# Transposes set inside the product ahead of them, later waits for joined branches, a rounding moved from GpSimd to VectorE, first refills in halves

## The reference

```python
h = _rmsnorm(x, g_mix[l])
rq, rk, rv, rg, nq, nk, nv, xq, gate_logits = jnp.split(h @ w_in[l], split_points, axis=-1)
y_ret = _retention_branch(rq, rk, rv, rg, ...)          # rotary q, k; (silu(rg) * group_norm(y)) @ w_ret_o
y_na = _neighbourhood_attention(nq, nk, nv, na_rpb[l]) @ w_na_o[l]
y_xa = _memory_cross_attention(xq, _rmsnorm(mem, g_mem[l]), w_mem_kv[l]) @ w_xa_o[l]
g_ret, g_na, g_xa = jnp.split(jax.nn.sigmoid(gate_logits), N_BRANCHES, axis=-1)
x = x + (g_ret * y_ret + g_na * y_na + g_xa * y_xa) @ w_out[l]
x = x + _hierarchical_moe(_rmsnorm(x, g_ffn[l]), ...)   # 4 groups x 4 experts, width 512, 2 per token
return _rmsnorm(x, g_final)
```

## Time and profile before

| what | value |
|---|---|
| median of 3 runs | 1771.41 us (1768.65 to 1774.07) |
| profiled execution, own time | 1773.05 us |
| its span, first to last instruction | 1771.3 us |
| PE busy | 1696.1 us (96%) |
| DVE, ACT, POOL busy | 326.0, 285.6, 64.7 us |
| DMA | 597.32 MB, mean 337 GB/s |
| mean granted clock of PE | 0.993 |

### The profile page before, as it was taken

How to read it: one execution, slowest core, us unless ns; L and a number is a source line. 1 busy time by engine, 2 the same in 40 slices (tenths; PEclk the granted TensorE clock), 3 DMA queues, 4 the chain that set the end, 5 groups by cost and what they waited for, 6 DMA issues and landing times.

```text
span 1771.3 us, 18844 instructions
## 1 busy us (share of the span) xinstructions
PE 1696.1 (96%) x8222; PEld 857.3 (48%) x8222; DVE 326.0 (18%) x770; ACT 285.6 (16%) x535; POOL 64.7 (4%) x92
## 2 busy tenths in 40 slices
PE   8999999989998999999998989999999999899996
PEld 7764443333433776543333333356544454565653
DVE  1340000000000325100000000031224132322222
ACT  2301110101010222110010101123240110122212
POOL 4000000000000101000000000040000000100000
PEclk9999999999999999999999999999999999899999
DMA  9878999999999936899999999995343426389996
GB/s 329 298 285 359 430 426 427 428 427 427 427 427 417 355 131 250 352 427 428 427 428 428 426 428 427 421 335 198 142 142 131 154 95 251 129 340 425 424 425 264
DMA packets 84498, 597.32 MB, mean 337 GB/s; under 512 B 5720, under 2 KB 14672, under 8 KB 51376
## 3 DMA queue, kind: packets, MB, share of 16 engines
q1 hardware_dynamic: 80848, 586.28, 81.5%
q0 software_dynamic: 3552, 9.65, 1.7%
HBM read 594.86 MB, written 1.05 MB: 336 GB/s over the span
## 4 chain that ended last, share of the span: by engine, by line
PE 66%; issue 18%; DMA 13%; DVE 1%; ACT 1%; POOL 0%; SPq 0%; POOLq 0%; DVEq 0%
PE psum L713 29%; PE psum L507 15%; DMA ring<-in_w_gate_dram 10%; PE psum L539 8%; DMA ring<-in_w_up_dram 3%; PE psum L701 3%; PE psum L746 2%; PE psum L546 2%; PE psum L566 1%; PE psum L662 1%; PE psum L579 1%; PE psum L594 1%; PE psum L767 1%; PE psum L499 1%; PE psum L606 0%
## 5 line engine op out<-in xcount | busy, mean ns | idle before, releaser
L713 PE MATMUL psum<-ring,xT 128*64 128x512 f32 (+1 forms) x2048 | 424.2, 562 | 35.6 <-DMA ring<-in_w_up_dram 18.8
L713 PEld LDWEIGHTS psum<-ring,xT 128*64 128x64 f32 x2048 | 147.0, 137 | 285.4 <-issue 248.9
L507 PE MATMUL psum<-ring,xT 128*128 128x512 f32 x592 | 258.5, 593 | 2.2 <-DVE work L2060 1.5
L713 PE MATMUL psum<-ring,work 128*64 128x512 f32 x1056 | 234.9, 593 | 2.9 <-ACT work L1355 1.4
L507 PEld LDWEIGHTS psum<-ring,xT 128*128 128x128 f32 x592 | 111.1, 190 | 136.9 <-issue 133.5
L1910 DVE TENSOR_TENSOR work<-work,psum 128x512 f32<-128x512 f32 (+1 forms) x48 | 43.5, 907 | 639.0 <-PE psum L713 639.0
L713 PEld LDWEIGHTS psum<-ring,work 128*64 128x64 f32 x1056 | 75.2, 137 | 147.6 <-issue 138.6
L539 PE MATMUL psum<-xT,ring 128*128 128x256 f32 x512 | 113.3, 380 | 1.5 <-DVE xT L1594 1.5
L1355 ACT COPY work<-psum 128x512 f32<-128x512 f32 (+1 forms) x48 | 24.7, 515 | 525.2 <-PE psum L767 525.2
L539 PEld LDWEIGHTS psum<-xT,ring 128*128 128x128 f32 x512 | 96.1, 190 | 15.0 <-DVE xT L1594 1.9
L1252 ACT ACTIVATE work<-psum 128x512 f32<-128x512 f32 (+1 forms) x86 | 49.5, 589 | 226.2 <-PE psum L507 119.0
(11 more groups left out here) (275 smaller groups left out, 1273.1 us busy)
## 6 DMA issues: line engine op xcount, KB each, us to landing
ring<-in_w_gate_dram SPq DMA_DIRECT2D x53, 2048.0 KB, 22.3
ring<-in_w_up_dram SPq DMA_DIRECT2D x53, 2048.0 KB, 24.4
ring<-in_w_down_dram SPq DMA_DIRECT2D x52, 2048.0 KB, 23.8
ring<-in_w_in_dram SPq DMA_DIRECT2D x16, 2048.0 KB, 9.7
ring<-in_w_exp_up_dram SPq DMA_DIRECT2D x16, 2048.0 KB, 20.6
ring<-in_w_exp_down_dram SPq DMA_DIRECT2D x11, 2048.0 KB, 22.3
work<-in_w_gate_dram SPq DMA_DIRECT2D x9, 2048.0 KB, 16.2
work<-in_w_exp_gate_dram SPq DMA_DIRECT2D x9, 2048.0 KB, 17.4
```

The source lines that it names most:

```text
L507: ins = pe.matmul(b[:, cols_at[0]:cols_at[1]], lhsT=lhsT(c), rhs=rhs(c), start=(c == order[0]), stop=(c == order[-1]))
L713: ins = pe.matmul(to[part * CAP:(part + 1) * CAP, 0:n], lhsT=lhsT, rhs=w[:, half * n:(half + 1) * n], start=first, stop=last)
```

## The change

Part 1, in block 2. `tile_around` is a product of one tile that calls `turns()` ahead of its chunk 6, so the transposes stand in the product's last quarter. It is used in three places: the turn of the normed input inside the product "xa", all four banks now of set v; the turn of y inside the last gate product, all of set v; and the turn of `comb` for t = 0 inside the third join, of set a (for t = 1 it stands between the first two tiles of "z", by `between`). The turns of q and k go ahead of the last "rg" tile, all of set a. `wait_made("joined")` of the second join now stands behind the rotary k's product; that of the third is replaced by waits for the tiles that a turn needs. DVE's and ACT's programs follow.

Part 2. `x_lo` is computed by DVE (`rounded_off`), and ACT's rounding `x_hi` moves ahead of its last copy.

Part 3, in all expert stages. The first refill that follows the first gate piece is loaded in halves: the first half when PE has done half of the piece's chunks (`half`), the second when all (`used`). To bring this forward the first gathers and the first gate chunks change order.

```diff
+            def tile_around(w, act, t, r, product, turns):
+                b = bank(r, product)
+                for c in range(DC):
+                    if c == 6:
+                        turns()
+                    ins = pe.matmul(b, lhsT=act[:, c, t * P:(t + 1) * P], rhs=w[:, c, :], start=(c == 0), stop=(c == DC - 1))
+                return full(r, ins)
...
-            freed[n] = nat(as_cols(n), memT, DC, 512, "a", "xa"); n += 1
-            turn(W(XA["H"], TC, D), DC, "xT", "mix")
+            w = as_cols(n)
+            tile(w, memT, DC, 512, 0, "a", "xa")
+            freed[n] = tile_around(w, memT, 1, "a", "xa", lambda: turn(W(XA["H"], TC, D), DC, "xT", "mix", rings="v")); n += 1
             wait_made("xT")
...
+            freed[n] = nat(as_cols(n), xT, DC, 512, "v", "rope"); n += 1
             wait_made("joined")
-            freed[n] = nat(as_cols(n), xT, DC, 512, "v", "rope"); n += 1
...
+            tile(as_cols(n), xT, DC, 512, 0, "a", "rg")
             wait_made("rope")
-            turn(W(RET["q"], TC, 512), 4, "rqk")
-            turn(W(RET["k"], TC, 512), 4, "rqk")
+            turn(W(RET["q"], TC, 512), 4, "rqk", rings="a")
+            turn(W(RET["k"], TC, 512), 4, "rqk", rings="a")
+            freed[n] = tile(as_cols(n), xT, DC, 512, 1, "a", "rg"); n += 1
...
-            turn(W(RET["y"], TC, D), DC, "oT", "gn")
+            tile(w, xT, DC, 512, 0, "a", "gate")
+            freed[n] = tile_around(w, xT, 1, "a", "gate", lambda: turn(W(RET["y"], TC, D), DC, "oT", "gn", rings="v")); n += 1
             wait_made("oT")
-            join(yT, DC, n); n += 2
-            wait_made("joined")
-            turn(W(W_COMB, TC, D), DC, "xT")
+            wait_made("gate")
+            freed[n] = nat(as_cols(n), yT, DC, 512, "v", "joined"); n += 1
+            w = as_cols(n)
+            tile(w, yT, DC, 512, 0, "v", "joined")
+            in_comb = made["joined_v"]
+            def comb_turned(t):
+                pe.wait_ge(S("joined_v"), in_comb + t)
+                turn(comb, DC, "xT", which=[t], rings="a")
+            freed[n] = tile_around(w, yT, 1, "v", "joined", lambda: comb_turned(0)); n += 1
...
+            def rounded_off(c):
+                dve.wait_ge(S("x_hi"), c + 1)
+                dve.tensor_tensor(x_lo[:, c, :], x[:, c, :], x_hi[:, c, :].bitcast(F32), ALU.subtract).then_inc(S("x_lo"), 1)
+            rounded_off(0)
+            turned_twice = lent[0] + 1
             b = borrow()
             dve.tensor_copy(xT[:, 0:4, P:2 * P], b.rearrange("p (a b) -> p a b", a=4)).then_inc(S("xT_v"), 1)
+            dve.wait_ge(S("a_full"), turned_twice)
+            rounded_off(1)
...
-                pool.tensor_tensor(x_lo[:, c, :], x[:, c, :], x_hi[:, c, :].bitcast(F32), ALU.subtract).then_inc(S("x_lo"), 1)
...
                     gather(0, 1, y_bank)
+                    pe.wait_ge(sem("xe"), plus(1, B["xe"]))
+                    up("gate", g_bank, 0, range(2))
                     gather(0, 2, u_bank)
                     pe.wait_ge(sem("xe"), plus(2, B["xe"]))
-                    up("gate", g_bank, 0, range(2))
+                    up("gate", g_bank, 0, range(2, 4))
                     gather(0, 3, m_bank)
-                    up("gate", g_bank, 0, range(2, 4))
                     pe.wait_ge(sem("xe"), plus(4, B["xe"]))
                     up("gate", g_bank, 0, range(4, DC))
...
+                    if early:
+                        sp.dma_start(ph.room(i)[:, 0:2048], half(0)).then_inc(sem("early"), 16)
+                        sp.wait_ge(sem("used"), B["used"] + 1)
+                        sp.dma_start(ph.room(i)[:, 2048:], half(1)).then_inc(sem("piece%d" % ph.place[i]), 16)
```

More of the change, by code:

```diff
@@ L325, in __init__ @@
                     self.landed.append(16 * uses[place])
+                self.split = self.last.index(0)
                 self.uses = {m: self.place.count(m) for m in order}
@@ L651, in by_tiles @@
                     for half, w in enumerate(ws):
+                        if between is not None and half != t:
+                            between() if half else wait_made("xT")
                         b = bank("v", product)
@@ L691, in experts, with gather @@
                 n_group = N_EXP // ph.group
-                def gather(g, part, to):
+                def gather(g, part, to, first=0, end=None):
                     pe.wait_ge(sem("pick"), plus(TC * (g + 1), B["pick"]))
@@ L697, in gather @@
                     terms = [(src, t) for t in range(TC) for src in ((x_hi, x_lo) if ph.group == 4 else (x,))]
-                    for c in range(n):
+                    for c in range(first, end or n):
                         at = (n * part + c) * P
@@ L707, in piece @@
                     pe.wait_ge(*ph.there(i, B))
+                    if i == ph.split and not ph.more:
+                        pe.wait_ge(sem("early"), B["early"] + 16)
                     return ph.room(i)
@@ L725, in up @@
                             ins.then_inc(sem("used"), 1)
+                        elif b == per // 2 - 1 and ph.at(matrix, e, q) == 0 and not ph.more:
+                            ins.then_inc(sem("half"), 1)
                 def down(e):
@@ L823, in experts @@
                     gather(0, 0, m_bank)
-                    gather(0, 1, y_bank)
+                    gather(0, 1, y_bank, 0, 2)
                     pe.wait_ge(sem("xe"), plus(1, B["xe"]))
-                    up("gate", g_bank, 0, halves[0])
+                    up("gate", g_bank, 0, range(2))
+                    gather(0, 1, y_bank, 2)
+                    up("gate", g_bank, 0, range(2, 4))
                     gather_next(-1)
@@ L1468, in _ @@
                 empty(W(XA["mv"], TC, 512)[:, c, :], "xa")
-            turn(xT, DC, "xT")
             qT = W(XA["qT"], 4, T)
@@ L1526, in _ @@
                 nat(v[:, :, half * 512:(half + 1) * 512], 512, "rv")
-            for half in range(2):
-                nat(rg[:, :, half * 512:(half + 1) * 512], 512, "rg", ACT.Silu)
-            turn(W(RET["qT"], 4, T), 4, "rqk")
-            turn(W(RET["kT"], 4, T), 4, "rqk")
+            nat(rg[:, :, 0:512], 512, "rg", ACT.Silu)
+            empty(rg[:, 0, 512:D], "rg", ACT.Silu)
+            for name in ("qT", "kT"):
+                for t in range(TC):
+                    empty(W(RET[name], 4, T)[:, :, t * P:(t + 1) * P], "rqk")
+            empty(rg[:, 1, 512:D], "rg", ACT.Silu)
             for h in range(RET_HEADS):
@@ L1535, in _ @@
                 nat(gate[:, :, half * 512:(half + 1) * 512], 512, "gate", ACT.Sigmoid)
-            turn(W(RET["yT"], DC, T), DC, "oT")
-            turn(xT, DC, "xT")
+            for t in range(TC):
+                for j in range(0, DC, 4):
+                    empty(xT[:, j:j + 4, t * P:(t + 1) * P], "xT")
             for c in range(TC):
@@ L1542, in _ @@
                 empty(xT[:, j:j + 4, 0:P], "xT")
+            for c in range(TC):
+                act.wait_ge(S("norm"), NORM_AT["ffn"] - TC + 1 + c)
+                act.copy(x_hi[:, c, :], x[:, c, :]).then_inc(S("x_hi"), 1)
             took[0] += 1
@@ L1545, in _ @@
             took[0] += 2
-            for c in range(TC):
-                act.wait_ge(S("norm"), NORM_AT["ffn"] - TC + 1 + c)
-                act.copy(x_hi[:, c, :], x[:, c, :]).then_inc(S("x_hi"), 1)
             routed(3)
@@ L2333, in load @@
                     i = ph.at(matrix, e, q)
-                    if ph.last[i] >= 0:
+                    early = i == ph.split and not ph.more
+                    if early:
+                        sp.wait_ge(sem("half"), B["half"] + 1)
+                    elif ph.last[i] >= 0:
                         sp.wait_ge(sem("used"), plus(ph.last[i] + 1, B["used"]))
@@ L2350, in load @@
                     else:
-                        for half, name in enumerate(("piece%d" % ph.place[i], "tail")):
-                            part = src[:, half] if src.shape[1] > 1 else src[:, 0, half * 2048:(half + 1) * 2048]
-                            sp.dma_start(ph.room(i)[:, half * 2048:(half + 1) * 2048], part).then_inc(sem(name), 16)
+                        for k, name in enumerate(("piece%d" % ph.place[i], "tail")):
+                            sp.dma_start(ph.room(i)[:, k * 2048:(k + 1) * 2048], half(k)).then_inc(sem(name), 16)
                 for q in range(ph.nq):
```

51 lines of the change are left out of this document (24 added, 27 removed).

## The result

The changed kernel takes 1760.01 us (median of 4 runs, 1758.17 to 1761.67), the kernel before beside it 1771.01 (4 runs, 1768.65 to 1774.07): a ratio of 0.9937, 95% interval 0.9924 to 0.995, or 11.0 us less. In a later comparison it was 1759.94 against 1770.43, ratio 0.9944 (0.9931 to 0.9958). Faster was right, and 1760.0 lies in the range. But the forecast of 1764.0 stood for 7.5 us, a third too little, so the question behind the result is which term was too small.

What follows compares the result with a forecast made beforehand. DMA bounds the expert stages, PE block 2, and a PE, DVE and ACT chain runs up to phase 2's first refill. 5.1 + 2.55 - 0.75 + 0.2 + 0.4 = 7.5 us gained, so 1764.0; range 1758.5 to 1769.5.

Steps and rivals of the forecast that it cites:

- Part 1: Block 2: PE's waits at turns and joins shrink or go, 5.1 us gained, bounds 4.0 and 6.0.
- Part 2: Router: without POOL's subtractions DVE's steps are short and the choice comes 2.55 us earlier, bounds 0.2 and 2.6.
- The new order of gathers: Phase 2: new PE wait for ACT behind the fourth gather part, 0.75 us lost; no wait added in phases 0 and 1.
- The halves: Expert stages' first refill: an earlier half piece gains 0.2 us in all, bounds -2.7 and 7.4.
- The gap is moved, not closed: Phase 0 stream: half a piece fills the dip at 142, but the stream then stands dry from about 147.
- the 7.4 of the upper bound: Most the halves could gain: 1.05 MB at 428 GB/s, 2.45 us in each of three expert stages.
- My condition for being wrong: Signs: phase 0 or 1 ends over 1 us earlier, DVE late for logits, or longer DMA waits in the last stage.
- Rival B: Expert stages: the earlier half starts the whole stream earlier, 2 us or more per stage, about 1758.5; 8%.
- The clock: Router: PE's idle stretch shrinks from 4.1 to 1.6 us; 0.4 us gained, bounds -1.7 and +3.1.
- Rival A: Router: PE's clock doesn't fall at all, giving 3.1 us instead of 0.4, so 1761.2; 25%.
- Rivals C and D: C: DVE's subtractions or moved waits cost more, about 1768, 12%. D: clock stays low into phase 2's experts, slower, 3%.
- The 1.6 us that I took off for the profiled execution: Profiled execution lies 1.6 us above the runs' median, so the forecast went from 1765.5 to 1764.0.

Runs made afterwards that it cites:

- no_gate_wait: Changed kernel without the wait for the last gate sigmoid ahead of the third join: 1757.48 us, ratio 0.993 to the kernel before.
- no_halves: Changed kernel with the first refills whole again, its new order of gathers kept: 1761.62 us, ratio 0.9947 to the kernel before.
- p1_waits: Kernel before with only the block 2 turns and joins changed: 1764.61 us, ratio 0.9965 to the kernel before.
- p3_halves: Kernel before with only the new order of gathers and gate chunks and the halved first refills: 1769.58 us, ratio 0.9998.
- p2_rounding: Kernel before with only x_lo's rounding moved to DVE: 1765.01 us, ratio 0.9969 to the kernel before.
- keep_4: Changed kernel with four filler matmuls instead of three ahead of the choice of experts: 1759.49 us, ratio 0.9942 to the kernel before.
- late_refill: Changed kernel with each expert stage's first refill issued only after PE used the second gate piece: 1773.68 us, ratio 1.002 to the kernel before.
- no_halves_again: Second timing of the changed kernel with whole first refills, new order of gathers kept: 1762.68 us, ratio 0.9955 to the kernel before.

## Why the prediction was right, and where its terms were off

**Part 1, forecast 5.1, measured 6.4.** The mechanism held at each place, only the size was off. From start to start, and the row of 1434.95 against the rows above: the first turn with the products around it (to 1190.08 and 1188.49) 0.97 (forecast 0.6), the second join 1.67 (1.51), the turns of q and k with retention behind them 1.08 (0.73), the turn of y 0.00 (0.04), the third join and the turn of `comb` 2.70 (2.24). Wherever a wait was closed it was worth more than the forecast, each time for the same reason. I added idle brackets, and a bracket begins where the last matmul's drawn end is. The 16 transposes are drawn 1.91 long, but with work behind them the next group starts after 1.75 (1170.36 to 1172.11); the prediction had both figures and still priced the waits by the bracket. With that tail a wait of 0.73 costs 0.89. The rest is in the group behind the wait, which takes 0.06 to 0.11 longer after a pause: 14.05 against 13.98 for the 64 records behind the first turn. Together that is 0.97, and no_gate_wait shows the same, 0.97 for 0.73, with 20.76 against 20.84 in the group behind. The five closed waits have 5.21 us in brackets, 0.8 in tails and 0.4 in slower starts, 6.4 in all. At the first turn I also had DVE's four copies too long. The bound of 6.0 was passed for these reasons.

**Part 2, forecast 2.55, measured 2.6.** Right in size and cause, though one stretched step of DVE was overlooked (0.75, above). POOL was the cause, each subtraction takes 1.2 us on DVE, both are covered, and PE's gap is 1.50 for 1.6.

**The new order of gathers, forecast 0.75 lost, measured 1.1 lost.** Right mechanism, and the bracket again as far as the 1.1 is explained. In phases 0 and 1 I said that no wait is added, and put the order at nothing. But SP issues the piece behind the split one 13.27 us after the first gather of phase 0 (148.98 in the changed kernel) and not 12.92 as before, 0.35 later, with halves and without. What this costs no run shows apart: phases 0 and 1 of no_halves are at most 0.14 longer than those of p1_waits, which has the old order.

**The halves, forecast 0.2 gained, measured 1.8 to 2.7.** This is the term that failed. "The gap is moved, not closed" was shown by the GB/s row, and the 7.4 of the upper bound never came. But I read the value of what is left from phase 0 alone, where the thin slices can be counted, and carried it to phase 2. There the stream gets a lead of 0.3 to 0.9 us, and PE's waits at the very end shrink by more. My condition for being wrong, phase 0 or 1 ending over 1 us earlier, looked at the wrong place: phase 0 ended 0.6 earlier in the changed kernel's profile and was 1.15 shorter, but p1_waits, without halves, was 1.20 shorter too. The fixed cost of some 2 us to each DMA that the Trainium skill gives, DMA: Bandwidth & Descriptors, section on the anatomy of one DMA, is stated there for DMAs that GpSimd issues, and SyncE issues the ones here; three extra DMAs gained time and did not lose 6 us, so it wasn't paid in the open. Rival B had the right sign of it and the right kind of evidence, the end of the stream, but not its mechanism: nothing was issued earlier behind the split piece, and it gave 2 us in each stage.

**The clock, forecast 0.4, measured about 1.1 by the profiles.** The term was too small, and its size stays rough. If I take of each profile how far the four router columns are above their shortest values, before, p1_waits and p3_halves, which round on POOL, lose 3.1, 1.7 and 0.9 us, mean 1.9; the eleven others lose between 0.1 and 1.7, mean 0.8. Three profiles against eleven, so 1.1 is rough; by its time p2_rounding gained 2.6 beyond the stretched steps, with an interval of 2 us either way. Rival A, that the clock stays up, came in 1 of 11 (keep_4), and low times were also seen before the positions. It is no property of this kernel but a chance in each execution. Rivals C and D didn't occur.

The sum of what the profiles measured is 6.4 + 2.6 - 1.1 + 2.4 + 1.1 = 11.4, against 11.0 and 10.5 by the times. The 1.6 us that I took off for the profiled execution was right in kind: its clock (3.1) was the worst of all fourteen, and its phase 0 the longest but for late_refill.

The errors didn't cancel. Part 1, the halves and the clock were forecast too low by 1.3, some 2 and 0.7 us, and against them stands only a loss forecast too low by 0.35. That 1760.0 still lies in the range, 1.5 us from its lower end, is in part luck: the room below the forecast had been made for rivals A and B, and neither came.

## What to carry to other kernels

Price a wait by the distance from start to start, against the same group with work behind it, not by the idle bracket; with five short waits closed here that was 1.2 us. If a change touches a stream that bounds a stage, look at the last waits of the stage, not at the slices around the edit: here a lead of half a microsecond was kept for 170 us, and delaying the refill on purpose shows in one run whether there is slack. Where an engine's short step is drawn ten times its length, look for the other engine whose long operation ends at the same time before touching the step.

## What the runs showed of the hardware

- A step of VectorE on 128 x 16 elements lasted 2.32 us (p1_waits) and one on 128 x 4 2.31 us (before), each until GpSimd's 128 x 1024 subtraction ended; with GpSimd idle they take 0.17 and 0.22. A reduction beside them kept its 0.16 us (1535.54 in before, 1528.90 in p1_waits).
- The same matmuls took 0.06 to 0.11 us longer behind a pause of 0.7 to 1.5 us than with work ahead of them (14.05 against 13.98 us, 20.84 against 20.76).
- The clock at the router fell at different places in executions of the same instructions, behind a gap of 1.5 us as well as behind 20-column matmuls that the profile shows as a busy PE. By the Trainium skill, TensorE: Matmul & The Clock Gate, section on what is actually happening, the same kernel can differ from run to run in how many of its matmuls run cold; the two profiles of the changed kernel agree (2.99 and 3.92 us to the positions).
- A wait of 2.87 us near the end cost another 1.5 us in the matmuls behind it through the clock (no_halves_again); a wait of 2.74 us at the same place in no_halves cost none, the clock stayed at 1.00, and neither did the waits of 1.1 us.
